# A decoder layer on one core: keys and values of the memory projected ahead of the first group of tokens

## The reference, cut to what matters

```python
def memory_kv(mem, g, w_k, w_v):
    mn = rmsnorm(mem, g)                       # (1, 256, 1024)
    return ((mn @ w_k).reshape(b, m, X_HEADS, X_HEAD_DIM),
            (mn @ w_v).reshape(b, m, X_HEADS, X_HEAD_DIM))   # both are outputs too
```

## Time and profile before

| | us |
|---|---|
| median of three runs | 1939.38 (1937.03 to 1941.72) |
| span of the profiled execution | 1935.6 |
| start to the first token panel | 0 to 18.9 |
| phases 0 to 2 | 18.9 to 424.9 |
| memory tiles made ready | 424.9 to 433.9 |
| chunks 6 and 7 with memory panels, then the last pair | 433.9 to 546.9 |
| samples | from 546.9 |

### The profile page before, as it was taken

One profiled execution on the slowest core, in us unless ns is written; L12 is line 12 of the kernel. 1 busy time (PEld: TensorE's weight loads), 2 busy tenths in 40 slices (PEclk: granted clock), 3 DMA queues, 4 the chain that ended last, 5 costly groups with the idle time before them and its releaser, 6 DMA issues. The chain is left out here.

```text
span 1935.6 us, 28162 instructions
## 1 busy us (share of the span) xinstructions
PE 1738.0 (90%) x10744; PEld 1641.0 (85%) x10744; DVE 909.5 (47%) x1189; ACT 758.2 (39%) x1378; POOL 132.0 (7%) x223
## 2 busy tenths in 40 slices
PE   7989888877856899999978889999999999999997
PEld 7978878866744898999964679999999999999996
DVE  3356666776433456444631344444334444355543
ACT  3454545454422345433521333333333333334432
POOL 1021111121010011000100000000000000000000
PEclk9989978889967899999998989999999999999998
DMA  6532222311222953422335244444334444346562
GB/s 176 129 83 73 65 77 77 74 56 57 86 89 77 257 160 97 131 77 79 117 99 208 87 142 128 122 132 137 114 107 152 129 130 134 112 122 199 169 178 69
DMA packets 393883, 227.72 MB, mean 118 GB/s; under 512 B 33715, under 2 KB 384031, under 8 KB 393778
## 3 DMA queue, kind: packets, MB, share of 16 engines
q1 hardware_dynamic: 393794, 226.51, 40.5%
HBM read 217.42 MB, written 10.07 MB: 118 GB/s over the span
## 5 line engine op out<-in xcount | busy, mean ns | idle before, releaser
L2568 DVE TENSOR_TENSOR f_wlo<-f_raw,f_whi 128x1024 fp32r<-128x1024 f32 (+1 forms) x180 | 239.7, 1332 | 368.4 <-ACT f_whi L2492 368.4
L2639 PE MATMUL f_bank<-next_hi,f_whi 128*128 128x384 f32 (+1 forms) x1056 | 342.7, 325 | 16.0 <-DVE f_wlo L2568 15.9
L2639 PE MATMUL f_bank<-next_hi,f_wlo 128*128 128x384 f32 (+1 forms) x1056 | 341.8, 324 | 0.0
L2639 PE MATMUL f_bank<-next_lo,f_whi 128*128 128x384 f32 (+1 forms) x1056 | 341.6, 323 | 0.0
L2492 ACT ACTIVATE f_whi<-f_raw 128x1024 fp32r<-128x1024 f32 (+1 forms) x180 | 205.5, 1142 | 236.7 <-PE f_bank L2639 231.5
L2639 PEld LDWEIGHTS f_bank<-next_hi,f_whi 128*128 128x128 f32 x1056 | 200.8, 190 | 17.3 <-issue 16.9
L2639 PEld LDWEIGHTS f_bank<-next_lo,f_whi 128*128 128x128 f32 x1056 | 200.8, 190 | 0.0
L2639 PEld LDWEIGHTS f_bank<-next_hi,f_wlo 128*128 128x128 f32 x1056 | 200.5, 190 | 0.0
L2639 PE MATMUL f_bank<-f_ahi,f_whi 128*128 128x384 f32 (+1 forms) x528 | 169.9, 322 | 0.3 <-DVE f_wlo L2568 0.3
L2639 PE MATMUL f_bank<-f_ahi,f_wlo 128*128 128x384 f32 (+1 forms) x528 | 169.4, 321 | 0.0
L2639 PE MATMUL f_bank<-f_alo,f_whi 128*128 128x384 f32 (+1 forms) x528 | 169.3, 321 | 0.0
(11 more groups left out here) (436 smaller groups left out, 3132.1 us busy)
## 6 DMA issues: line engine op xcount, KB each, us to landing
f_raw<-w_gate SPq DMA_DIRECT2D x66, 512.0 KB, 3.7
f_raw<-w_up SPq DMA_DIRECT2D x66, 512.0 KB, 3.7
f_raw<-w_down SPq DMA_DIRECT2D x48, 704.0 KB, 4.6
a_raw<-w_in SPq DMA_DIRECT2D x114, 256.0 KB, 3.2
b_raw<-w_xq SPq DMA_DIRECT2D x24, 512.0 KB, 4.1
b_raw<-w_xo SPq DMA_DIRECT2D x24, 512.0 KB, 3.9
xm<-x_prompt SPq DMA_DIRECT2D x16, 512.0 KB, 4.9
b_raw<-w_out SPq DMA_DIRECT2D x24, 256.0 KB, 3.8
```

What stands on the lines that cost most here:

```text
L2568: dve.tensor_tensor(w_lo[:, s % 2, 0:kt], raw[:, s, 0:kt], w_hi[:, s % 2, 0:kt].bitcast(F32), ALU.subtract)\
L2639: ins = pe.matmul(out, a[:, s % 2, k, :], b[:, k0 + k, 0:w], start=(first and k == 0 and m == 0), stop=(last and k == kt - 1 and m == 2))
```

## The change

The memory comes first. SP loads tiles 9 and 10 and the memory's gain (into `rr`, so that `gpre` is loaded once), then the sixteen memory panels, with the constants, `gpre` and token tiles 0 to 2 between them. All panels are renumbered: 0 to 15 are the memory's, and `first_panel(g)` gives the start of a group. `turn(t)` is the place of tile t in the new order. Phase 3 is left with chunks 6 and 7 alone. `mem_kv` keeps its place, so group 1's evictions and POOL's halo copy wait until it has been stored, now by two DMAs during group 0.

```diff
+def first_panel(g):
+    return NMP + NPA * g
+def turn(t):
+    return t + 2 if t < 9 else t - 9
...
+        gmem = rr[:].rearrange("p h n -> p (h n)")
...
# SP
-            sp.dma_start(xt(0), x_rows(0)).then_inc(x_full[0], 16)
-            sp.dma_start(gpre[:], row("g_mix_pre").broadcast_to([P, D])).then_inc(gpre_in, 16)
+            for m in range(2):
+                sp.dma_start(hn[m][:], io["mem_prompt"][0, P * m:P * m + P, :]).then_inc(mem_full[m], 16)
+                if m == 0:
+                    sp.dma_start(gmem, row("g_mem").broadcast_to([P, D])).then_inc(gmem_in, 16)
...
+            for n in range(NMP):
+                if n == 3:
+                    for dst, src in loads:
+                        sp.dma_start(dst, src).then_inc(consts_in, 16)
+                    sp.dma_start(gpre[:], row("g_mix_pre").broadcast_to([P, D])).then_inc(gpre_in, 16)
+                if n in (4, 6, 8):
+                    load_x((n - 4) // 2)
+                load_panel(n)
             for g in range(3):
...
+                    if g == 0 and n == first_panel(0) + 4:
+                        for a, name in ((0, "p_mem_k"), (1, "p_mem_v")):
+                            sp.wait_ge(S["evac_done"], ready(KT * a + KT - 1))
+                            sp.dma_start(io[name][0, 0].rearrange("(m p) h d -> p m (h d)", p=P), mem_kv[:, a])\
+                                .then_inc(mem_stored, 16)
...
-                    if n == NPA * 2 + 4:
-
-                        sp.wait_ge(S["hn_done"], ready(8))
-                        sp.dma_start(gpre[:], row("g_mem").broadcast_to([P, D])).then_inc(gmem_in, 16)
-                        load_x(9)
-                        load_x(10)
...
# ACT, evac of a token panel
+                if g == 1:
+                    act.wait_ge(mem_stored, 32)
...
# ACT, start
+            norm(9)
+            norm(10)
+            norm_evac(9)
+            split_hi(0, 0, 0, 32)
+            norm_evac(10)
+            split_hi(1, 1, 1, 32)
+            for n in range(NMP):
+                mem_evac(n)
+                if n in (9, 11, 13):
+                    norm((n - 9) // 2)
             for t in range(3):
-                norm(t)
...
+                norm_evac(t)
...
# ACT, DVE and PE, phase 3 (PE's lines)
-                    else:
-                        mem_panel(MEM0 + 6 * i + k)
...
-                    pe.wait_ge(S["hlo_done"], ready(2 * 10 + 1))
                     slots(gp, gb, 0, False)
                     slots(gp, gb, 1, True)
-                    for n in range(MEM0 + 12, NPANELS_1):
-                        mem_panel(n)
...
# DVE, start
+            norm(9)
+            norm(10)
+            norm_evac(9)
+            split_lo(0, 0, 0)
+            norm_evac(10)
+            split_lo(1, 1, 1)
+            for n in range(NMP):
+                mem_lo(n)
+                if n in (11, 13):
+                    norm((n - 11) // 2)
             norm_evac(0)
...
# PE, start
+            norm(9)
+            norm(10)
+            pe.wait_ge(S["hlo_done"], ready(2 * turn(10) + 1))
+            for n in range(NMP):
+                mem_panel(n)
             for t in range(3):
                 norm(t)
```

More of the change, by code:

```diff
@@ L155, in build_mixers @@
         mem_kv = proj[:, 1].rearrange("p k n -> p (k n)")[:, 0:4 * D].rearrange("p (a m n) -> p a m n", a=2, m=2)
-        x_in = lambda t: xt(t) if t < 9 else hn[t % 2][:]
+        x_in = lambda t: xt(t) if t < 9 else hn[turn(t) % 2][:]
+        x_loads = lambda t: 16 * (t // 3 + 1) if t < 9 else 16
+        gmem = rr[:].rearrange("p h n -> p (h n)")
         square_out = residual[:, 2, 2 * D:3 * D]
@@ L172, in build_mixers @@
         x_full = [sem(f"x_full{n}") for n in range(3)]
+        mem_full = [sem(f"mem_full{n}") for n in range(2)]
+        x_landed = lambda t: x_full[t % 3] if t < 9 else mem_full[t - 9]
         gpre_in, consts_in, consts_done, gmem_in, mem_stored = sem("gpre_in"), sem("consts_in"), sem("consts_done"), sem("gmem_in"), sem("mem_stored")
@@ new lines, in _ @@
+            for g in range(3):
+                for n in range(first_panel(g), first_panel(g + 1)):
+                    if g == 0 and n == first_panel(0) + 4:
[3 more added lines that the diff above has]
+                                .then_inc(mem_stored, 16)
+                    if g < 2 and n in (first_panel(g) + 6, first_panel(g) + 8, first_panel(g) + 10):
+                        load_x(3 * g + 3 + (n - first_panel(g) - 6) // 2)
+                    load_panel(n)
@@ L282, in _ @@
+            sp.wait_ge(mem_stored, 32)
         @block.gpsimd
@@ L289, in _ @@
                 k += 1
-            for gb in range(2):
-                pool.memset(proj[:, gb, 0:8, 0:3], 0.0).then_inc(consts_done, 1)
-                k += 1
+            pool.memset(proj[:, 0, 0:8, 0:3], 0.0).then_inc(consts_done, 1)
+            k += 1
             pool.wait_ge(consts_done, k)
@@ L347, in chunk @@
                 pool.tensor_tensor(rsu[:], rsu[:], mhalf[:, 0:2], ALU.pow).then_inc(S["ur_done"], 1)
-            for t in range(3):
+            for t in (9, 10, 0, 1, 2):
                 norm(t)
@@ L354, in _ @@
                     if g < 2:
-                        pool.wait_ge(S["evac_done"], ready(NPA * g + 1 + T_XBC + 7))
+                        pool.wait_ge(S["evac_done"], ready(first_panel(g) + 1 + T_XBC + 7))
+                        pool.wait_ge(mem_stored, 32)
                         pool.wait_ge(consts_done, k)
@@ L363, in _ @@
                 if ph < 3:
-                    for t in range(3 * ph + 3, 3 * ph + (6 if ph < 2 else 5)):
+                    for t in range(3 * ph + 3, 3 * ph + 6 if ph < 2 else 9):
                         norm(t)
@@ L383, in norm @@
                 r = group_rows(t)
-                act.wait_ge(x_full[t % 3], 16 * (t // 3 + 1))
-                act.wait_ge(S["sumsq_done"], ready(t - 1))
+                act.wait_ge(x_landed(t), x_loads(t))
+                act.wait_ge(S["sumsq_done"], ready(turn(t) - 1))
                 act.activation(square_out[0:r, :], x_in(t)[0:r, :], ACT.Square, accum_out=ss[0:r, t:t + 1])\
@@ L389, in norm_evac @@
             def norm_evac(t):
-                r, g = group_rows(t), t // 3
+                r = group_rows(t)
                 c0 = 128 * (t % 3)
                 for h in range(2):
-                    act.wait_ge(S["hT_done"], ready(2 * t + h))
-                    act.wait_ge(S["panel_done"], ready(NPA * g - 1))
+                    act.wait_ge(S["hT_done"], ready(2 * turn(t) + h))
+                    act.wait_ge(S["panel_done"], ready(first_panel(t // 3) - 1 if t < 9 else -1))
                     act.activation(h_hi[:, 4 * h:4 * h + 4, c0:c0 + r],
@@ L526, in slots @@
                             dt_part(gp, k)
-                        if k >= 3 and (gp < 2 or k < 5):
+                        if k >= 3 and gp < 2:
                             norm(3 * gp + k)
@@ L594, in _ @@
                     slots(gp, gb, 2, True)
-                    for t in range(3 * gp + 3, 3 * gp + (6 if gp < 2 else 5)):
+                    for t in range(3 * gp + 3, 3 * gp + 6 if gp < 2 else 9):
                         norm_evac(t)
@@ L614, in norm @@
                 r = group_rows(t)
-                dve.wait_ge(S["rstd_done"], ready(t))
-                dve.wait_ge(S["hT_done"], ready(2 * t - 3))
+                q = turn(t)
+                dve.wait_ge(S["rstd_done"], ready(q))
+                dve.wait_ge(S["hT_done"], ready(2 * q - 3))
+                dve.wait_ge(gpre_in if t < 9 else gmem_in, 16)
                 if t >= 9:
-                    dve.wait_ge(gmem_in, 16)
-                    dve.wait_ge(x_full[t % 3], 16 * (t // 3 + 1))
-                dve.scalar_tensor_tensor(hn[t % 2][0:r, :], x_in(t)[0:r, :], rs[0:r, t:t + 1], gpre[0:r, :], ALU.mult, ALU.mult)\
+                    dve.wait_ge(x_landed(t), 16)
+                dve.scalar_tensor_tensor(hn[q % 2][0:r, :], x_in(t)[0:r, :], rs[0:r, t:t + 1],
+                                         gpre[0:r, :] if t < 9 else gmem, ALU.mult, ALU.mult)\
                     .then_inc(S["hn_done"], 1)
@@ L626, in norm_evac @@
                 for h in range(2):
-                    dve.wait_ge(S["hhi_done"], ready(2 * t + h))
+                    dve.wait_ge(S["hhi_done"], ready(2 * turn(t) + h))
                     dve.tensor_tensor(h_lo[:, 4 * h:4 * h + 4, c0:c0 + r],
@@ L854, in slots @@
                             attended(gb, i, 1)
-                    if last and gp < 3 and k == 5:
+                    if last and gp < 2 and k == 5:
                         norm(3 * gp + 3)
@@ L919, in norm @@
                 r = group_rows(t)
-                cl = 3 * (t // 3) - 4
-                pe.wait_ge(S["hn_done"], ready(t))
+                cl = 3 * (t // 3) - 4 if t < 9 else -4
+                q = turn(t)
+                pe.wait_ge(S["hn_done"], ready(q))
                 for h in range(2):
-                    pe.wait_ge(S["hlo_done"], ready(2 * t + h - 2))
```

(13 more changed lines are left out.)

73 lines of the change are left out of this document (20 added, 53 removed).

## The result

The changed kernel takes 1982.28 us (median of four runs, 1975.24 to 1987.20) where the kernel before took 1940.14 (four runs on the same chip): a ratio of 1.0221, 95% interval 1.0195 to 1.0247. It is slower by 42 us. The forecast was 1983.0.

The account below looks back on a forecast made before the run. PE was taken as filled by panels among the chunks, bare at the end, where splits leave an uncovered gap. Front +93.7 less tail 50 gave +43.7 on 1935.6, 1979.3; with 3.8 around the span, 1983 us, range 1963 to 1999.

Parts of the forecast that it names:

- bounds for front and tail: First group's start delayed 80 to 100 us; samples' first DMA brought forward 47 to 56 us.
- Front: Kernel's start: eight uncovered memory bursts, then three token tiles; first group starts at 112.6 instead of 18.95, 93.7 us later.
- one bare pair: Last memory pair before the samples, with nothing beside it: 9.43 us burst to burst, 3.7 of them an uncovered gap.
- dearer price: Memory pair paying both the 3.7 us gap and the slow clock behind it: 11.85 us; mean taken as 11.0.
- B: Rival for the front: PE's clock stays up, a pair takes 9.43 us, +30, 1969 us; chance 0.12.
- C: Rival for the front: the clock never rises, a pair takes 13.95 us, +66.5, 2006 us; chance 0.06.
- both prices: Between memory pairs: a 3.7 us gap while PE waits for splits, then a slow-clock burst of 8.15 us instead of 5.75.
- Rival E: Front: next pair's splits hide beneath the matmuls, so not slower; with the shortest tail +1, 1940 us; chance 0.05.
- Stores and constants: Front: constant loads covered by the first burst; two 1 MB key and value stores cost 0, up to 3 us uncovered.
- Tail: Last two chunks without memory work: together 71 us, samples' first DMA at 497 instead of 546.96, 50 us earlier.
- rival D: Tail: panels merely fill idle time, chunks keep their time, only 34 us returned; +60, 2000 us; chance 0.07.
- panels on the path (33) or off it (50): Chunk 6, 50.3 us before: 33 left if all six panels lay on its path, 50 if none; 37 to 41 expected.

Follow-up runs that it names:

- first experiment: Changed kernel with a second pair of weight buffers for the front's memory panels, odd pairs in two other PSUM banks: 1943.37 us, ratio 1.0023 to the kernel before.
- second experiment: Changed kernel with 28 unread matmuls added on PE after each memory pair but the last: 1971.66 us, ratio 1.0169 to the kernel before.
- third experiment: Changed kernel with twelve memory panels' matmuls, unread, put back into the last two chunks' steps: 1989.05 us, ratio 1.0258 to the kernel before.
- last experiment: Kernel before with a second pair of weight buffers in the tail and splits moved one step earlier: 1925.64 us beside 1934.85, ratio 0.9948.
- last two experiments: Kernel before with a second pair of weight buffers in the tail: 1938.35 us, ratio 0.9985; the same with splits one step earlier: 1925.64 us, ratio 0.9948.

## Why the prediction was right

- **The number.** Forecast and median differ by 0.7 us, and the forecast of the span, 1979.3, was met to the tenth. So close a hit is luck, since the four runs spread over 12 us. The stated range has a slip: the bounds for front and tail give 1963 to 1992, not 1999; the result lies inside either.
- **Front.** Predicted 17.2 + 7 x 11.0 + 8 + 10.4 = 112.6. Measured 16.95, a first burst of 7.8, 7 x 11.29, and 9.9 for the three tiles: 113.7. The one bare pair of before showed the mechanism that all seven pairs repeat, and the choice of 11.0 near the dearer price was right: behind the gaps the clock was at its lower level, and it rose within the burst (rivals B and C out). The value was a judgement, not worked out, and 11.85 was no upper bound: the second pair took 12.08.
- **What makes the pair dear.** Of 11.29 us, 5.75 are matmuls at the full clock, 3.6 the wait, 1.9 the slow start. The first experiment takes away both prices and the second the slow start alone, and the first token panel follows each (77.26 and 102.35 for 113.73). Rival E's condition, splits beneath the bursts, was tried by the first experiment: 1943 us, where E's sum said 1940.
- **Stores and constants.** The stores were issued at 107.14 and 107.69 and took 5.3 and 7.5 us, so they had landed by about 115, with no wait charged to them; 0 was right.
- **Tail.** Predicted 50 us back, measured 50.7, and chunks 6 and 7 in 69.3 us where I said 71. The size was right in part by luck: the way to chunk 6's first scores gave 11.7 us where I had 13.2, and the shorter chunks made up for it. The clock of the chunks was to be mostly 0.50 and was 0.71 and 0.79. And one reason was wrong. I argued against rival D that "a chunk's small products do queue behind panels", and bounded chunk 6 by panels on the path (33) or off it (50). The third experiment puts the matmuls back and chunk 6 stays at 40.7. D's premise, that PE's panel work fills idle time, was nearly true. D's consequence, chunks that keep 50 us, was false, since a panel is more than its matmuls: its splits stand in the lists of ACT and DVE, and PE waits for them. So D and I made the same mistake with opposite signs. Of the 50.7 us, 21.2 were the last two pairs (525.76 to 546.96; chunk 7's last step on ACT ends at 526.2), some 6.5 the matmuls (2.5 of them ahead of chunk 6's first scores), and 9 the rest of that way, mostly the memory tiles. Of the 14 left, the last experiment takes back 8.6 (13.6 less the bare end's 5.0) by moving the splits; the runs don't divide the remainder.
- **The closing sentence of the sum**, that PE work was taken "out from under chains that left PE room, and put where nothing covers their splits", is what the runs show, more than the bounds of 33 and 50 us for chunk 6.

## What to carry to other kernels

Before moving work from a covered place to a bare one, look for the place where the trace already shows one unit of it bare, and price the move by that unit, the slow clock behind its gap included. Then ask whether the unit's engine time or its hand-over is dear: here 34.5 us of matmuls cost 6.5 in and ahead of the chunks, while a split in the wrong place of a list cost a wait of up to 4.3 us each time. A second buffer helps only if the instruction that fills it also stands early enough in its engine's list (0.15% against 0.5%).

## What the runs showed of the hardware that I had not expected

The very first burst of the changed kernel is slow while the page grants it the full clock (PE's window from its first matmul):

```profile
16.95:21.00 4.05, 4.05 (x19) 1.00 1.03 328
```

Nineteen matmuls in 4.05 us are 0.21 us each, the spacing that goes with 0.50 in the rows above. So I go by the spacing there; why the clock column says 1.00 is open.

And a kernel that is the same in a stretch need not take the same time in it. Around the step from group 0 to group 1, where the last two experiments change no work, their executions lost 3.4 us, most of it here. PE's windows in the kernel before, and in the last experiment:

```profile
120.00:125.00 5.00, 3.54 (x21) 0.98 0.00 0
125.00:130.00 5.00, 5.00 (x31) 1.00 0.00 0
```

```profile
120.00:125.00 5.00, 3.59 (x14) 0.50 0.00 0
125.00:130.00 5.00, 5.00 (x21) 0.64 0.00 0
```

The same stretch in the changed kernel, and in the second experiment, which changes nothing behind the memory pairs:

```profile
215.00:220.00 5.00, 3.59 (x21) 0.95 0.00 0
```

```profile
204.00:209.00 5.00, 3.59 (x14) 0.50 0.00 0
```

The clock rose a few us later behind the same idle stretch. Such shifts are as large as the effects of some edits here, so small gains are better measured from a common point in the trace as well as by the whole time. What decided when it rose was not tried.
